# Two modulation tiles moved from the first down projection to the wait for the second norm (Trainium2, one core)

## The reference

```python
mod = (silu(c) @ w_ada + b_ada).reshape(B, 9, 1, 1024)      # sh1 sc1 g1 sh2 sc2 g2 sh3 sc3 g3
h = x + 0.5 * g1 * swiglu(rmsnorm(x) * (1 + sc1) + sh1, ffn_up[0], ffn_down[0])
h = h + g2 * (W_out[ GDN(hn) ++ MoBA(hn) ]),  hn = rmsnorm(h) * (1 + sc2) + sh2   # one projection W_in feeds both
h = h + 0.5 * g3 * swiglu(rmsnorm(h) * (1 + sc3) + sh3, ffn_up[1], ffn_down[1])
y = rmsnorm(h)
```

## Time and profile before

| | us |
|---|---|
| median of 3 runs | 932.88 (927.55, 933.91, 932.88) |
| the profiled execution | 927.22 |
| its span, first to last instruction | 925.6 |
| PE busy | 859.5 (93%) |
| DVE, ACT, GpSimd busy | 501.3, 304.6, 113.9 |
| mean granted TensorE clock | 0.983 of full speed |
| moved by DMA | 204.83 MB, mean 221 GB/s |

### The profile page before, as it was taken

How to read it: one execution, slowest core, us unless ns; L and a number is a source line. 1 busy time by engine, 2 the same in 40 slices (tenths; PEclk the granted TensorE clock), 3 DMA queues, 4 the chain that set the end, 5 groups by cost and what they waited for, 6 DMA issues and landing times.

```text
span 925.6 us, 19660 instructions
## 1 busy us (share of the span) xinstructions
PE 859.5 (93%) x7464; PEld 751.7 (81%) x7464; DVE 501.3 (54%) x961; ACT 304.6 (33%) x499; POOL 113.9 (12%) x197
## 2 busy tenths in 40 slices
PE   4889999999999999999999848998899999999996
PEld 3789999998997999966656524665777999999996
DVE  1445454543355667566656566657446565544363
ACT  1333333332323336453434511000225334432331
POOL 2000000000021000132223223230130000000021
PEclk9999999999999999999999988999999999999999
DMA  9999979785755252378778698898391555434401
GB/s 323 370 307 357 308 255 312 253 320 185 300 199 182 92 182 59 125 243 268 230 232 289 205 369 289 296 333 311 87 338 57 167 182 176 145 137 156 159 1 51
DMA packets 122163, 204.83 MB, mean 221 GB/s; under 512 B 7548, under 2 KB 56982, under 8 KB 121970
## 3 DMA queue, kind: packets, MB, share of 16 engines
q1 hardware_dynamic: 104976, 163.08, 50.9%
q0 software_dynamic: 11648, 38.45, 12.4%
q10 hardware_dynamic: 5474, 2.39, 1.0%
HBM read 199.01 MB, written 4.88 MB: 220 GB/s over the span
## 4 chain that ended last, share of the span: by engine, by line
PE 83%; DVE 5%; DMA 4%; issue 2%; ACTq 2%; ACT 2%; POOL 1%; POOLq 1%; DVEq 0%; SPq 0%
PE bank L741 19%; PE bank L743 18%; PE bank L742 18%; PE bank L704 8%; PE bank L1015 3%; PE bank L1251 3%; PE bank L723 3%; PE bank L1055 2%; DMA kv<-in_cache_v 2%; ACTq L1515 2%; DMA wring<-in_w_ada 1%; DMA region<-in_x_sample 1%; DVE wring_rounded L1590 1%; PE bank L1200 1%; PE bank L1187 1%
## 5 line engine op out<-in xcount | busy, mean ns | idle before, releaser
L741 PE MATMUL bank<-hn_rounded,kv_rounded 128*128 128x288 f32 x928 | 276.7, 298 | 5.9 <-DVE wring_rounded L1590 4.1
L742 PE MATMUL bank<-xs_rounded,kv_rounded 128*128 128x288 f32 x928 | 274.4, 296 | 0.0
L743 PE MATMUL bank<-hn_rounded,wring_rounded 128*128 128x288 f32 x928 | 273.6, 295 | 0.0
L1590 DVE TENSOR_TENSOR wring_rounded<-wring,kv_rounded 128x1024 fp32r<-128x1024 f32 (+1 forms) x164 | 188.3, 1198 | 71.7 <-ACT kv_rounded L1311 71.6
L1311 ACT CAST kv_rounded<-wring 128x1024 fp32r<-128x1024 f32 (+1 forms) x164 | 158.5, 1026 | 162.0 <-PE bank L743 109.7
L741 PEld LDWEIGHTS bank<-hn_rounded,kv_rounded 128*128 128x128 f32 x928 | 174.4, 188 | 10.2 <-DVE wring_rounded L1590 4.7
L743 PEld LDWEIGHTS bank<-hn_rounded,wring_rounded 128*128 128x128 f32 x928 | 175.4, 189 | 0.0
L742 PEld LDWEIGHTS bank<-xs_rounded,kv_rounded 128*128 128x128 f32 x928 | 174.9, 189 | 0.0
L741 PE MATMUL bank<-region_rounded,kv_rounded 128*128 128x288 f32 x352 | 105.5, 300 | 1.6 <-DVE modT L1582 1.6
L742 PE MATMUL bank<-region_rounded,kv_rounded 128*128 128x288 f32 x352 | 104.6, 297 | 0.0
L743 PE MATMUL bank<-region_rounded,wring_rounded 128*128 128x288 f32 x352 | 104.2, 296 | 0.0
(11 more groups left out here) (275 smaller groups left out, 987.4 us busy)
## 6 DMA issues: line engine op xcount, KB each, us to landing
wring<-in_ffn_up SPq DMA_DIRECT2D x44, 1024.0 KB, 7.7
wring<-in_w_ada SPq DMA_DIRECT2D x36, 1024.0 KB, 10.9
wring<-in_ffn_down SPq DMA_DIRECT2D x16, 1024.0 KB, 7.3
kv<-in_cache_v SPq DMA_DIRECT2D x64, 256.0 KB, 4.9
kv<-in_cache_v POOLq DMA_DIRECT2D x64, 256.0 KB, 5.2
wring<-in_w_in SPq DMA_DIRECT2D x14, 1024.0 KB, 6.4
kv<-in_cache_k SPq DMA_DIRECT2D x44, 256.0 KB, 4.5
kv<-in_cache_k POOLq DMA_DIRECT2D x44, 256.0 KB, 4.8
```

The source lines that it names most:

```text
L741: nc.tensor.matmul(out, hi, rhs_hi, start=start, stop=False)
L742: nc.tensor.matmul(out, hi, rhs_lo, start=False, stop=False)
L743: return nc.tensor.matmul(out, lo, rhs_hi, start=False, stop=stop)
L1590: v.tensor_tensor(wringR[:, slot, c, :], wring[:, slot, c, :], whiR[:, u % 2, c, :], ALU.subtract).then_inc(s_wlo, 1)
```

## The change

The order of loads puts the six down tiles together and modulation tiles 16 and 17 behind them, ahead of the input tiles. PE multiplies both after the two sums of the second norm, where the spare products stood (and no longer waits there for the second part of the constants), and transposes them after the first input tile; it waits for the adds at turn 6. ACT's two copies move behind `norm(1)`. DVE's two adds move between `norm(1)` and the rests of the second input tile; the first residual and the second norm now wait for 16 modulation tiles. GpSimd clears `adasb` after the squares.

```diff
-        tiles += [("down", 0, 0, 0), ("ada", 16), ("down", 0, 0, 1), ("ada", 17), ("down", 0, 0, 2)]
-        tiles += [("down", 0, 1, t) for t in range(3)]
+        tiles += [("down", 0, g, t) for g in range(2) for t in range(3)]
+        tiles += [("ada", 16), ("ada", 17)]
         tiles += [("in", j) for j in range(7)]
...
             square(0)
+            pool.wait_ge(s_pt, 16)
+            square_sum(1)
             pool.wait_ge(s_adaT, ADA_TILES)
             pool.memset(adaf[:], 0.0).then_inc(s_qz, 1)
-            pool.wait_ge(s_pt, 16)
-            square_sum(1)
             first_k_steps(pool, 1)
...
-                        if l == 0 and g == 0 and t == 0:
-                            ada_mm(16, *tile(("ada", 16)), bank=0)
-                        elif l == 0 and g == 0 and t == 1:
-                            ada_T(16, 0, bank=2)
-                            ada_mm(17, *tile(("ada", 17)), bank=1)
-                        elif l == 0 and g == 0:
-                            ada_T(17, 1, bank=3)
-                            pe.wait_ge(s_modr, ADA_TILES)
...
             sumsq(1)
-            pe.wait_ge(s_cst2, 16)
-            spare_products(4)
+            ada_mm(16, *tile(("ada", 16)), bank=5)
+            ada_mm(17, *tile(("ada", 17)), bank=6)
             for k in range(KD):
...
+            ada_T(16, 0, bank=7)
+            ada_T(17, 1, bank=6)
             for turn in range(4, 29):
+                if turn == 6:
+                    pe.wait_ge(s_modr, ADA_TILES)
...
             for u in range(UP_TILES + 1, IN0 + 1):
                 round_quarters(u, range(4))
-                if u < UP_TILES + 3:
-                    j = 16 + u - UP_TILES - 1
-                    act.wait_ge(s_adamm, j + 1)
-                    act.wait_ge(s_adaT, j - 1)
-                    nc.scalar.copy(adasb[:, j % 2, 0:P], ps[j % 2][:, 0:P]).then_inc(s_adaev, 1)
             norm(1)
+            for j in range(16, ADA_TILES):
+                act.wait_ge(s_adamm, j + 1)
+                act.wait_ge(s_adaT, j - 1)
+                nc.scalar.copy(adasb[:, j % 2, 0:P], ps[j - 11][:, 0:P]).then_inc(s_adaev, 1)
...
-                    dve.wait_ge(s_modr, ADA_FIRST if ni == 0 else ADA_TILES)
+                    dve.wait_ge(s_modr, (ADA_FIRST, 16, ADA_TILES)[ni])
...
-            rest_quarters(UP_TILES + 2, range(4))
-            mod_tile(16, 0, bank=2)
-            rest_quarters(UP_TILES + 3, range(4))
-            mod_tile(17, 1, bank=3)
-            rest_quarters(UP_TILES + 4, range(4))
-            dve.wait_ge(s_modr, ADA_TILES)
+            for u in range(UP_TILES + 2, UP_TILES + 5):
+                rest_quarters(u, range(4))
+            dve.wait_ge(s_modr, 16)
             residual(0, (UP_TILES + 5, IN0))
             norm(1)
+            mod_tile(16, 0, bank=7)
+            mod_tile(17, 1, bank=6)
             rest_quarters(IN0 + 1, range(4))
```

## The result

| | before | after |
|---|---|---|
| median of 22 executions each, us | 931.59 (926.41 to 939.98) | 935.50 (931.85 to 942.07) |
| ratio, 95% interval | | 1.0045 (1.0025 to 1.0065) |
| profiled execution, us | 927.22 (span 925.6) | 942.07 (span 940.4) |

The changed kernel is slower by 4.2 us, 2.3 to 6.1 (0.45% of 931). The forecast was 937.5 in 930.9 to 944.4, +7.3 us. The profiled execution of after is the slowest of its 22 and that of before one of the quicker, so the 14.8 us between the two spans is not the effect.

What follows compares the result with a forecast made beforehand. PE was taken as the bound, with 83% of the chain that ended last. A later first input product (+4.4 us) and DVE's order (+2.9) gave +7.3 on a base of 930.2: 937.5, range 930.9 to 944.4.

Steps and rivals of the forecast that it cites:

- Part 1: Down stage: with the two modulation tiles and the add wait gone, 4.8 us less PE time before the last two down tiles.
- Part 2: Loads: the first input tile (in0) is asked for only at 277.7, lands 8.1 us later; the norm's sums move 3.15 us later.
- The fit that gave 6.8 us: Skill's estimate for in0's 2 MB load: fixed 2.0 us plus bytes at 436 GB/s; 1.3 us less delay; not used.
- Part 3: Wait before the second norm's sums: clock falls to 0.50, back 3.6 us after PE resumes; first input product +4.4 us.
- (a): Wait before the norm's sums: the clock does not fall; +6.05 us, 936.3; chance 0.13.
- (b): Clock stays low through both modulation tiles, and the pause behind in0's products lowers it again; +10.5 us, 940.7; chance 0.15.
- Part 4: Behind in0's products: DVE's adds precede the second input tile's rests, so PE waits; +2.9 us, bounds 2.6 and 3.9.
- The sum: Delay at the norm, +4.4 us, and behind in0's products, +2.9 us, together +7.3 us.
- I expect the delay to reach the end: After the input stage: later loads and pages are released by PE's reads of input tiles, so +7.3 us reaches the end.
- Rival (d): A later stage, waiting for pages and not PE, gives half the delay back: +3.7 us, 933.9; chance 0.12.
- Rival (c): in0 is not what the norm waits for: -1.9 us (928.3), or -4.8 (925.4) with DVE's wait covered; chance 0.08.
- Within 1%: Whole kernel: change in time stays inside about 1% (9.3 us), called same; chance 0.66, slower 0.31, faster 0.03.

Runs made afterwards that it cites:

- the spare products: Changed kernel plus ten spare products in PE's idle time ahead of the two sums; ratio to the kernel before 1.0055 (1.0029 to 1.0080).
- the two more profiles: The changed kernel, nothing altered, profiled and measured twice more against the kernel before: ratios 1.0055 and 1.0090.
- the third: The changed kernel measured a third time, on the chip where the kernel before is measured against itself: ratio 1.0090 (1.0061 to 1.0119).
- the 24 spare products: Kernel before plus 24 spare products on PE between the second norm's first chunk and the first input product, a plain delay: ratio 1.0194 (1.0156 to 1.0231).
- in0 first: Changed kernel with the first input tile (in0) loaded ahead of the two modulation tiles: ratio to the kernel before 0.9976 (0.9947 to 1.0004).

## Why the prediction was right, and where not

- **Part 1, the down stage.** Forecast 4.8 us less. In after the down tile before the last ends at 278.79, 62.6 us behind the first down product; before it was 67.5 (282.48 - 214.94): 4.9 us.
- **Part 2, the late load.** Forecast: asked for when that tile is read, awaited until 8.1 us later, sums 3.15 us later. Measured: asked for at 278.87, rounding from 287.00, 8.1 us; the sums moved from 78.8 to 82.1, 81.9 and 81.9, +3.1 to +3.3. The fit that gave 6.8 us stands in the Trainium skill (DMA: Bandwidth & Descriptors, Anatomy of one DMA) for transfers that GpSimd issues, and in0's are issued by SP: it bore on them less than the prediction says.
- **Part 3, the clock.** Forecast: low, back 3.6 us after PE resumes, first input product +4.4, of which 1.25 is the clock. Measured: +4.5, and the spare products give 1.4 for the clock. The 128 modulation records took 4.28 us (4.74 and 4.53 in the two more profiles, forecast 4.5), and the sums 2.29 (forecast 2.05); in after the two misses nearly cancel. One reading behind the forecast does not hold: the row at 14.54 that gave 3.37 us for 64 records at the low level stands where the granted clock reads 1.00 (14 to 18). Measured, 128 records took 3.70 at 1.00 and 4.74 with some 2.2 us of them at 0.50, so some 0.5 us lost per us. Rivals (a) and (b) are out for the changed kernel, though the second half of (b), a fall in the pause of part 4, did come in the profile of the spare products. In this trace the Trainium skill's rule (TensorE: Matmul & The Clock Gate, HAM oscillation: a wait for a transfer leaves the next burst cold) holds, with 0.50 behind a wait of 9.96 us that goes back to in0's transfer.
- **Part 4, DVE's order.** Forecast +2.9. Measured 2.7 by turning that order back, or 2.9 as what after loses between the first input product and the softplus step (90.0 against 87.1). Its low bound, 2.6, was near.
- **The sum.** Forecast +7.3 at the end of the input stage; measured +7.4, +7.6 and +7.4 in three profiles.
- **From there to the end.** "I expect the delay to reach the end" is the step that the times alone do not settle. The first measurement gave 4.2 us (2.3 to 6.1), which leaves out 7.4; the third 8.4 (5.7 to 11.1); all three together 5.5. Rival (d), half given back, would give 3.7, and the 24 spare products speak against a share of that size (18.0 of 19.8 arrived). A fixed loss of 1 to 2 us for any delay would fit both. So would scatter: no change at all measured 1.6 us. The estimate at like clock, 7.0 and 7.8 us, speaks for scatter, and for a delay that arrives whole. A loss of 1 us or so stays possible.
- **The forecast time.** That 935.50 lies only 2.0 us under 937.5 is in part luck: the base was set at 930.2 and measured 931.59, which hides 1.4 us of what the first measurement of the effect falls short.
- **Rival (c)**, the faster side, was out as the loads stood: in0 is asked for at 278.9 and not before 269.6. With in0 first it holds: sums 4.9 us sooner than before (with the 1.5 added), and the ratio is 0.9976 with DVE's order as changed and 0.9937 without, where the rival gave -1.9 and -4.8 us (0.998 and 0.995).
- **The chances.** "Within 1%" came true in all three measurements, though the interval of the third (1.0061 to 1.0119) reaches past it.

## What to carry to other kernels

When a step is moved, write down the list of loads behind it and count back by the depth of the ring: at the full clock the two tiles cost nothing where they now stand (in0 first), but being ahead of in0 in a ring of four they made its load land some 8 us behind the moment at which ACT could have begun with it. In a program that an engine runs in order, a small step that waits for another engine belongs behind the large ones that do not wait: two adds of 0.3 us together held 4.6 us of ready work, at a cost of 2.7 us. And a long gap that opens on TensorE has a second price behind it, the clock; if it cannot be closed, work that nobody reads can fill it, which brought the first input product 1.4 us sooner here, of which 0.6 was left at the softplus step. Where the end scatters by more than the effect, a stretch between two marks and the granted clock of each execution tell more than another median.

## What the runs showed of the hardware

- The scatter of this kernel goes in large part with the granted clock. Over the 22 executions of after the time correlates with the time at the low level (twice one minus the mean clock, times the time) at 0.80: it runs from 34 to 53 us, and with each of these the time is about 0.4 us longer. In the twelve other sets of executions (the other kernels, and the kernel before beside them) the correlation is 0.77 to 0.94 and the slope 0.30 to 0.56.
- The clock can be low behind a short pause too. Ahead of the down stage PE makes a modulation tile, a transpose, and waits 1.28 us; in 7 of the 11 profiles 0.50 follows, at a price of 1.5 us, and in the other four it does not, with the same instructions on PE up to there. What decides is not shown: each of the two kernels with more than one profile showed it every time.
- The two 1 MB halves of an input tile, alone in the queue, took 8.1 us from the first issue to the start of the work that waits for both (278.87 to 287.00).
